# Moving the norm of two attention heads and half of the output projection into the end of the attention loop

## What is computed

```python
proj = rms_norm(x) @ w_in          # lru_x, lru_gate, q, k, v: 512 columns each
y_lru = rglru_group(lru_x, lru_gate, ...)     # short convolution, gates, a scan over time, gelu
w = softmax(q1 @ k1.T) - lam * softmax(q2 @ k2.T)   # causal, 4 heads, 2 x 64 of q and k each
o = w @ v                          # 128 values per head
y_att = rms_norm(o) * head_gain * 0.8
x = x + rms_norm(concat(y_lru, y_att) @ w_out)
x = x + rms_norm(relu(rms_norm(x) @ w_up)**2 @ w_down)
```

## Time and profile before

| | |
|---|---|
| median of 3 runs | 1195.84 us (1195.27 to 1197.99) |
| the profiled execution | 1198.78 us |
| its span, first to last instruction | 1197.0 us |
| PE busy | 1161.9 us, 97% |
| DVE, ACT busy | 641.8 us (54%), 395.6 us (33%) |
| mean granted PE clock | 0.989 of full speed |

### The profile page before, as it was taken

How to read it: one execution, slowest core, us unless ns; L and a number is a source line. 1 busy time by engine, 2 the same in 40 slices (tenths; PEclk the granted TensorE clock), 3 DMA queues, 4 the chain that set the end, 5 groups by cost and what they waited for, 6 DMA issues and landing times.

```text
span 1197.0 us, 13587 instructions
## 1 busy us (share of the span) xinstructions
PE 1161.9 (97%) x5236; PEld 938.4 (78%) x5236; DVE 641.8 (54%) x848; ACT 395.6 (33%) x666; POOL 34.6 (3%) x47
## 2 busy tenths in 40 slices
PE   7999899999978999999999999999999999999997
PEld 6888787777655788878888888888888888888886
DVE  6666745755743646744444444444444544544458
ACT  7434723545554236641121121122122112112122
POOL 0300000000010100200000000000000000000000
PEclk9999999999988999999999999999999999999999
DMA  6111223112100354021111121121011111111112
GB/s 231 43 36 62 103 90 91 42 36 53 53 1 1 128 168 144 1 88 53 36 55 51 35 70 37 34 70 53 33 55 53 53 35 53 53 35 53 53 53 105
DMA packets 21094, 74.74 MB, mean 62 GB/s; under 512 B 2832, under 2 KB 2960, under 8 KB 20928
## 3 DMA queue, kind: packets, MB, share of 16 engines
q1 hardware_dynamic: 17568, 63.45, 15.9%
q0 software_dynamic: 1664, 6.49, 1.6%
q10 hardware_dynamic: 1824, 4.29, 1.6%
HBM read 65.82 MB, written 4.19 MB: 58 GB/s over the span
## 4 chain that ended last, share of the span: by engine, by line
PE 91%; DVE 4%; ACT 2%; issue 1%; DMA 1%; SPq 0%; ACTq 0%; DVEq 0%
PE pair L307 27%; PE pair L309 27%; PE pair L308 27%; PE pair L616 3%; PE pair L649 3%; PE pair L633 1%; PE pair L619 1%; DMA raw<-weights 1%; DVE negmax L1408 1%; PE pair L465 1%; PE pair L688 1%; ACT wh L863 0%; PE pair L658 0%; ACT dec L944 0%; DVE probs L1402 0%
## 5 line engine op out<-in xcount | busy, mean ns | idle before, releaser
L1595 DVE TENSOR_TENSOR yacc<-yacc,pair 128x1024 f32<-128x1024 f32 x112 | 136.7, 1220 | 133.0 <-PE pair L309 133.0
L307 PE MATMUL pair<-yh,wh 128*128 128x512 f32 x512 | 199.6, 390 | 1.9 <-DVE yl L1522 1.2
L309 PE MATMUL pair<-yh,wl 128*128 128x512 f32 x512 | 199.2, 389 | 0.0
L308 PE MATMUL pair<-yl,wh 128*128 128x512 f32 x512 | 199.2, 389 | 0.0
L308 PE MATMUL pair<-wdl,xh 128*128 128x512 f32 x480 | 187.0, 390 | 0.0
L307 PE MATMUL pair<-wdh,xh 128*128 128x512 f32 x480 | 187.0, 390 | 0.0
L309 PE MATMUL pair<-wdh,xl 128*128 128x512 f32 x480 | 186.8, 389 | 0.0
L1583 DVE TENSOR_TENSOR relu<-relu 128x512 f32<-128x512 f32 x64 | 44.3, 692 | 213.4 <-ACT xh L1164 213.4
L863 ACT ACTIVATE wdh<-raw 128x1024 fp32r<-128x1024 f32 x30 | 30.3, 1053 | 278.5 <-PE pair L309 274.4
L1232 DVE TENSOR_TENSOR wl<-raw,wh 128x1024 fp32r<-128x1024 f32 x70 | 85.4, 1221 | 61.4 <-ACT wh L863 61.4
L1161 ACT ACTIVATE relu<-pair 128x512 f32<-128x512 f32 x64 | 38.3, 598 | 228.8 <-PE pair L309 228.8
(11 more groups left out here) (208 smaller groups left out, 1464.5 us busy)
## 6 DMA issues: line engine op xcount, KB each, us to landing
raw<-weights SPq DMA_DIRECT2D x104, 512.0 KB, 3.3
x_sb<-x SPq DMA_DIRECT2D x8, 512.0 KB, 7.7
q_rot<-q_sb ACTq DMA_DIRECT2D x32, 128.0 KB, 2.4
out<-h_sb SPq DMA_DIRECT2D x7, 512.0 KB, 2.6
x_a<-x POOLq DMA_DIRECT2D x4, 512.0 KB, 5.6
x_b<-x POOLq DMA_DIRECT2D x4, 512.0 KB, 6.9
cos_t<-rope POOLq DMA_DIRECT2D x1, 1024.0 KB, 5.1
gw_raw<-gate_weights POOLq DMA_DIRECT2D x1, 512.0 KB, 3.6
```

What stands on the lines that cost most here:

```text
L307: pe.matmul(o, a_hi, b_hi, start=first, stop=False)
L308: pe.matmul(o, a_hi, b_lo, start=False, stop=False)
L309: return pe.matmul(o, a_lo, b_hi, start=False, stop=last)
L1595: dve.tensor_tensor(y, y, pair[2 + t % 2][:, :], ALU.add).then_inc(y_added, 1)
```

## The change

Five things change.

- **Second half of the values.** ACT makes the high part of piece P_VB ahead of the four square roots of the scan instead of behind them, and that of P_VB+1 ahead of the value copies. DVE makes the low parts one place earlier in its scan loop.
- **Norm of heads 0 and 1 inside the last head's steps.** At step 21 DVE adds epsilon for 16 of the 32 columns and ACT takes their roots; at steps 24 and 25 DVE makes the reciprocals and the diagonals; at steps 25 to 28 PE spreads one half of a head per step into bank 4, and DVE multiplies it (`spread_half`, `early_norm`). ACT copies the high parts at steps 28 and 30, DVE subtracts the low parts at steps 29 and 31. The diagonals of these heads lie in memory of their own.
- **Low parts of P_OUT and P_OUT+1.** DVE makes them at steps 26 and 27 instead of 18 and 22.
- **First step of each head.** At s = 8, 16 and 24 DVE now combines the step before ahead of taking the new maxima.
- **Recurrent half of the output projection, quarter 0.** Its 48 matmuls are cut in four parts of 12 (`out_part`): ahead of the last step's transposes, behind its value products, and around the last sum of squares. Only the spreads of heads 2 and 3 stay behind the attention, now between the two chunks of j = 2. ACT loads the square root's table at s = 32 by a small operation.

```diff
-        diag = sb("diag", [P, 2, T], F32, at_s)
+        diag = [sb("diag01", [P, 2, T], F32, at_x + 40 * KB), sb("diag23", [P, 2, T], F32, at_s)]
...
+        head_mix = [28, 30]
+
+
+        EARLY_NORM = 2 * TT
+        spread_at = [25, 26, 27, 28]
...
+                if j >= EARLY_NORM // 2:
+                    pe.wait_ge(head_var, 1)
...
+            def spread_half(h, hf):
+
+                pe.wait_ge(diag_done, h + 1)
+                pe.wait_ge(q_copied, UNITS)
+                if h + hf:
+                    pe.wait_ge(o_norm_half, 2 * h + hf)
+                pe.matmul(bank(4), ones[:, :], diag[0][:, h, HALF * hf:HALF * hf + HALF], start=True,
+                          stop=True).then_inc(spread_done, 1)
+
+            def out_part(j, tiles):
+
+                pe.wait_ge(w_lo, P_OUT + j + 1)
+                pe.wait_ge(lru_mixed, LC)
+                for kk in range(2):
+                    k = 2 * j + kk
+                    w_cols = slice(HALF * kk, HALF * kk + HALF)
+                    for t in tiles:
+                        if k == 0:
+                            pe.wait_ge(exped, 2 * (steps - 1) + t // 2 + 1)
+                        tok = slice(P * t, P * t + P)
+                        mm = mm3(pe, bank(t), xh[:, mixed_slot(k), tok], xl[:, mixed_slot(k), tok], wh[j][:, w_cols],
+                                 wl[j][:, w_cols], k == 0, False)
+                return mm
...
                     score_step(s)
                 project(filler)
+                if s in spread_at:
+                    spread_half(*divmod(spread_at.index(s), 2))
+                if s == steps:
+                    out_part(0, (0, 1))
...
+            out_part(0, (2, 3)).then_inc(piece_used, 1)
             sumsq_step(steps // 2 - 2)
             for part in range(2):
                 pv_step(steps // 2 - 1, part)
+            out_part(1, (0, 1))
             sumsq_step(steps // 2 - 1)
+            out_part(1, (2, 3)).then_inc(piece_used, 1)
...
 
...
-                if h >= 2:
-                    pe.wait_ge(o_norm, h - 1)
+                pe.wait_ge(o_norm_half, 4)
...
-            for quarter in range(3):
+            for j in range(2, 4):
+                pe.wait_ge(w_lo, P_OUT + j + 1)
+                for kk in range(2):
+                    pe.wait_ge(mix_lo, 2 * j - 4 + kk + 1)
+                    if j == 2 and kk == 1:
+                        spread(2)
+                        spread(3)
+                    token_piece(j % 2, j, range(4), 0, None, mixed_slot, (kk,))
+            for quarter in range(1, 3):
                 for j in range(4):
                     pe.wait_ge(w_lo, P_OUT + 4 * quarter + j + 1)
-                    if quarter == 0:
-
-                        if j < 2:
-                            pe.wait_ge(lru_mixed, LC)
-                        else:
-                            pe.wait_ge(mix_lo, 2 * j - 2)
-                        if j == 1:
-                            spread(0)
-                            spread(1)
-                        if j == 2:
-                            spread(2)
-                            spread(3)
...
                     hi_early(P_VA + 2 + c)
+            hi_early(P_VB)
             for c in range(LC):
                 act.wait_ge(bsq_done, c + 1)
                 act.activation(u_t[:, c, :], u_t[:, c, :], ACT.Sqrt).then_inc(sqrt_done, 1)
-            hi_early(P_VB)
...
             act.wait_ge(rstd_ready, 1)
+            hi_early(P_VB + 1)
             v_copies(0)
-            for j in range(1, N_V):
+            for j in range(2, N_V):
...
+            def head_roots(n):
+
+                cs = slice(EARLY_NORM * n, EARLY_NORM * n + EARLY_NORM)
+                act.wait_ge(head_var, n + 1)
+                act.activation(hroot[:, cs], hvar[:, cs], ACT.Sqrt).then_inc(head_root, 1)
...
                 if s < steps:
                     exp_step(s)
+                else:
+                    act.activation(root[:, 0:1], ones[:, 0:1], ACT.Sqrt)
...
+                if s == EARLY_NORM + 5:
+                    head_roots(0)
+                if s in head_mix:
+                    h = head_mix.index(s)
+                    act.wait_ge(o_norm_half, 2 * h + 2)
+                    act.activation(xh[:, h, :], qk(2 * h), ACT.Copy).then_inc(head_hi, 1)
...
+            hi_early(P_OUT + 2)
             o_step(steps // 2 - 1)
-            act.wait_ge(head_var, 1)
-            act.activation(hroot[:, :], hvar[:, :], ACT.Sqrt).then_inc(head_root, 1)
-
-            for h in range(HEADS):
-                if h % 2 == 0:
-                    hi_early(P_OUT + 2 + h // 2)
-                act.wait_ge(o_norm, h + 1)
-                act.activation(xh[:, h, :], qk(2 * h), ACT.Copy).then_inc(mix_hi, 1)
+            head_roots(1)
+            hi_early(P_OUT + 3)
+            for h in range(2, HEADS):
+                act.wait_ge(o_norm, h - 1)
+                act.activation(xh[:, h, :], qk(2 * h), ACT.Copy).then_inc(head_hi, 1)
...
+            lo_early(P_VB)
...
+                lo_early(P_VB + 1 + c)
                 dve.wait_ge(scan_step, 2 * c + 2)
                 dve.wait_ge(gelu_done, LC)
                 dve.tensor_tensor(gel[:, c, :], u_t[:, c, :], gel[:, c, :], ALU.mult).then_inc(lru_done, 1)
-                lo_early(P_VB + c)
-            lo_early(P_QK)
...
+            def head_vars(n):
...
+                dve.wait_ge(sumsq_done, EARLY_NORM // 2 * (n + 1))
+                dve.wait_ge(o_copied, EARLY_NORM // 2 * (n + 1) + 1 - n)
+                dve.scalar_tensor_tensor(hvar[:, cs], head_sums[:, cs], 1.0 / P, sum0_eps[:, cs], ALU.mult,
+                                         ALU.add).then_inc(head_var, 1)
+
...
+            def diagonals(h):
+                for t in range(TT):
+                    ins = dve.tensor_scalar(diag[h // 2][:, h % 2, P * t:P * t + P], ident[:, :],
+                                            hrstd[:, TT * h + t:TT * h + t + 1], None, ALU.mult)
+                ins.then_inc(diag_done, 1)
+
+            def early_norm(s):
+
+                if s == EARLY_NORM + 5:
+                    head_vars(0)
+                if s == EARLY_NORM + 8:
+                    dve.wait_ge(qk_bank, UNITS)
+                    head_rstd(0)
+                    diagonals(0)
+                if s == EARLY_NORM + 9:
+                    diagonals(1)
+                if s in spread_at:
+                    n = spread_at.index(s)
+                    h, hf = divmod(n, 2)
+                    q = qk(2 * h)[:, HALF * hf:HALF * hf + HALF]
+                    dve.wait_ge(spread_done, n + 1)
+                    dve.scalar_tensor_tensor(q, q, head_gain[:, 0:1], bank(4), ALU.mult,
+                                             ALU.mult).then_inc(o_norm_half, 1)
+                if s - 1 in head_mix:
+                    h = head_mix.index(s - 1)
+                    dve.wait_ge(head_hi, h + 1)
+                    dve.tensor_tensor(xl[:, h, :], qk(2 * h), xh[:, h, :].bitcast(F32),
+                                      ALU.subtract).then_inc(mix_lo, 1)
+
...
-                max_first = s < steps and s % TT < TT // 2 and s % 2 == 0
+                max_first = s < steps and 0 < s % TT < TT // 2 and s % 2 == 0
...
+                    if s == (unit_end(2 * n + 1) + 1 if n < 6 else 20 + n):
+                        lo_early(P_QK + n + 2)
                     if s == unit_end(2 * n + 1) + 1:
-                        lo_early(P_QK + n + 2)
                         rope_cos(n)
...
-            link(dve.tensor_tensor(sum0_eps[:, :], sum0[:, :], sum0[:, :], ALU.mult))
-            link(dve.tensor_scalar(sum0_eps[:, :], sum0_eps[:, :], EPS, None, ALU.mult))
-            dve.wait_ge(sumsq_done, steps // 2)
-            dve.scalar_tensor_tensor(hvar[:, :], head_sums, 1.0 / P, sum0_eps[:, :], ALU.mult,
-                                     ALU.add).then_inc(head_var, 1)
-            dve.wait_ge(head_root, 1)
-            rsqrt_post(hvar[:, :], hroot[:, :], ht1[:, :], ht2[:, :], hrstd[:, :])
...
-            def diagonals(h):
-                if h >= 2:
-                    dve.wait_ge(spread_done, 2 * (h - 1))
...
-            for h in range(0, HEADS, 2):
-                diagonals(h)
-                diagonals(h + 1)
-                lo_early(P_OUT + 2 + h // 2)
-                for n in range(h, h + 2):
-                    dve.wait_ge(spread_done, 2 * n + 2)
-                    dve.scalar_tensor_tensor(qk(2 * n), qk(2 * n), head_gain[:, 0:1],
-                                             pair[2 + n % 2][:, :], ALU.mult, ALU.mult).then_inc(o_norm, 1)
-                for n in range(h, h + 2):
-                    dve.wait_ge(o_norm, n + 1)
-                    dve.wait_ge(mix_hi, LC + n + 1)
-                    dve.tensor_tensor(xl[:, n, :], qk(2 * n), xh[:, n, :].bitcast(F32),
-                                      ALU.subtract).then_inc(mix_lo, 1)
+                early_norm(s)
+
+            lo_early(P_OUT + 2)
+            head_vars(1)
+            head_rstd(1)
```

(12 more changed lines are left out.)

23 lines of the change are left out of this document (15 added, 8 removed).

## The result

The changed kernel takes 1185.87 us (median of 4 runs, 1184.89 to 1186.3), the kernel before, on the same chip in the same minutes, 1196.85 us (1195.27 to 1197.99). The ratio is 0.9909, with a 95% interval of 0.9897 to 0.9921: 11.0 us faster. Forecast was 1185.6 us. The profiled execution took 1185.46 us.

A forecast was written before the change was run, and what follows sets the result against it. PE was taken as the bound, 91% of the last-ending chain over 1197.0 us. Terms -4.9 + 4.0 - 5.0 - 1.1 - 3.6 + 0.4 = -10.2 us, off the median 1195.84, gave 1185.6 us; range 1181.0 to 1191.0.

The forecast's parts named there:

- Values, -4.9: Second half of the values: PE's wait for P_VB's low part and the half clock behind it go, -4.9 us.
- The rival that the wait only moves: At the values, P_VB+1 is late instead, so the 4.9 us are not won: 1190.5 us, chance 0.04.
- Roots at step 21, +2.8: Two table loads and a root delay step 22's exp and so PE's scores of step 23: +2.8 us.
- drain: Rival at the table switches: each holds ACT for longer than its load, 2.6 us more, 1188.2 us; chance 0.02.
- Step 24, -1.3: At step 24 the combine of step 23 goes ahead of the maxima and PE gets it earlier: -1.3 us.
- The clock of the loop, +0.6: PE's longer idle at step 22 may cost clock: +0.6 us, between 0 and 1.7.
- Spreads, +1.9, and the low parts at nothing: Steps 25 to 28: PE's spread halves cost +1.9 us; DVE's low parts fit where it waits anyway.
- The loop in all, +4.0: Whole last-head loop: 2.8 - 1.3 + 1.9 + 0.6 = +4.0 us, with ends 0 and +8.
- Behind the last scores, -5.0 and -1.1: Behind the last scores, moved matmuls fill PE's four gaps, -5.0 us, and the half-clock loss goes, -1.1 us.
- Spreads off the path, -3.6, changes of matmul kind, +0.4: Heads 0 and 1 spreads leave PE's path behind the attention, -3.6 us; four more matmul-kind changes cost +0.4.
- The cover that goes: Norm chain of heads 2 and 3 has less matmul cover but just fits, margins 0.3 and 0.2 us.
- Half clock through the last head, 0.05: Rival: PE stays at half clock from 324.14 to 375 us, +18 us, total 1203 us; chance 0.05.

The follow-up runs named there:

- experiment 1: The kernel before with only the new order of the value pieces (P_VB and P_VB+1 made earlier on ACT and DVE): 1189.45 us.
- experiment 3: The changed kernel with the epsilon and roots of heads 0 and 1 at step 20 instead of 21: 1182.94 us.
- experiment 7: The changed kernel with the low parts of P_OUT and P_OUT+1 at steps 18 and 22 again, as before: 1183.75 us.
- experiment 6: The changed kernel with the maxima ahead of the combine again at steps 8, 16 and 24: 1188.12 us.
- experiment 11: The changed kernel with eight useless matmuls added on PE behind each of steps 22 and 23: 1187.80 us; its profiled run 1183.15 us.
- Experiment 4: The changed kernel with GpSimd's four recurrent low-part subtractions cut to 8 of 1024 columns each, output less exact: 1182.02 us.
- Experiment 2: The changed kernel with the four parts of the recurrent half put back behind the last sum of squares: 1192.18 us.
- experiment 5: The kernel before with the new value order and the four recurrent parts moved, but all four heads normed behind the attention: 1194.43 us.
- experiment 8: The changed kernel with roots at step 20, low parts at 18 and 22, and ACT's recurrent copies at 22, 25, 26, 27: 1179.18 us.
- experiments 9: The kernel before with the new value order alone, plus four useless matmuls on PE behind each of steps 22 to 30: 1192.91 us.

## Why the prediction was right, and where not

The total was right to 0.3 us of the measured median, and sign and range held; none of the rivals came as a whole. Term by term:

- *Values, -4.9:* right. 4.98 us in the change's trace; 5.0 in experiment 1's at the values, though only 3.7 of them at step 22; -4.9 at equal clock. The rival that the wait only moves is refuted: PE has no wait there.
- *Roots at step 21, +2.8:* right in kind. The load at 318.94 starts 0.01 us behind ACT's copy and the operation behind each load at most 0.02 us behind it, so no drain shows on either side. Scores 23 came 3.8 us late against step 22: a DMA issue of ACT ahead of the exp took 1.46 us, 0.85 more than in the kernel before and in experiments 3 and 7, which the prediction could not know. That the median of experiment 3 gives 2.9 us back is near the term partly by luck, since its roots at step 20 still cost 0.8 us.
- *Step 24, -1.3:* right. PE's wait went from 2.12 to 0.79 us, and experiment 6 gives 1.5 at equal clock.
- *The clock of the loop, +0.6:* **the step that failed.** I priced the longer wait alone, from the gap at the values. Behind the 4.94 us of idle, scores, transposes and products took 3.7 us more than at full clock (4.77, 1.72 and 2.68 against 2.97, 0.95 and 1.54 in experiment 11). Half of it went into the 2.08 us that PE waited there before; 1.8 us reached scores 24 (10.01 us from scores 23 on, 8.20 in experiment 11). After that the clock was 1.00 for the rest of the head, and this I had at nothing: the kernel before takes 38.2 us from the transposes of step 23 to the last value products, the same instructions of experiment 1 take 33.8, and 1.4 us of those are half clock at their start (3.51 us up to scores 25, for 2.11 in the change). So a clock of 1.00 throughout is worth some 5.8 us there, an estimate. Both are larger than the term, and opposite.
- *Spreads, +1.9, and the low parts at nothing:* **mis-sized.** I asked only whether DVE was free, not who else worked then. Eight diagonals, a weight's low part and a head's low part fell beside GpSimd, and PE had two new waits of 1.1 us for DVE. Experiment 4 prices this at 3.9 us, 3.65 of them in this stretch; experiment 7 prices the moved low parts at 2.1, part of it the same loss. The spreads themselves were cheaper than forecast: without GpSimd the stretch takes 32.96 us with them, and 33.8 less 1.4 without them at full clock, so about 0.5 us, an estimate.
- *The loop in all, +4.0:* 2.7 in the profiled pair, which is 3.8 (exp) + 1.8 (half clock at scores 23) - 1.3 (step 24) - 5.8 (better clock later) + 0.5 (spreads) + 3.7 (GpSimd). So the near hit is luck: two costs and one larger gain that nobody forecast almost cancel. The gain is not the change's own to claim, since experiment 1 has most of it without a single spread.
- *Behind the last scores, -5.0 and -1.1:* right. Experiment 2 undoes it for 6.3 us.
- *Spreads off the path, -3.6, changes of matmul kind, +0.4:* the tail gained 10.8 us in all where -9.3 was the sum. The estimate of 0.1 for a change of kind holds: behind the first matmul of each of the four parts the next starts 0.31 to 0.33 us later, for 0.23 within a part. The slow clock of before was worth 1.5 us, not 1.1 (20.4 us from the last value products of the loop to the first spread, for 18.9 in experiment 1). The rest, some 0.7 us, is not split up.
- *The cover that goes:* right, with more room than I had worked out: 0.75 us ahead of the spreads. That the cover matters is what experiment 5 shows from the other side.
- *Half clock through the last head, 0.05:* did not come. Its place was right; a window at 0.62 is there, but the clock was back at 1.00 from 335 us on.

The total itself needs the same caution. The medians differ by 11.0 us, the kernels at equal clock by 9.6, the profiled pair by 13.3: a forecast of 10.2 is right by each of them to about 3 us, and to 0.3 us only by the first.

Of the signs named ahead, the one on scores 23 came out otherwise: 3.8 us later against step 22, not 2.8; and quarter 0 ended 13 us earlier in the profiled pair, not 10.

## What to carry to other kernels

Before moving work into an engine's idle time, look at who else is active in that window, not only at whether the engine is free: here four short GpSimd instructions took 3.9 us from a change worth 11. Work that fills one gap can have been the cover of another, as in experiment 5; look what it covered before moving it. And when kernels differ by a few us with PE partly idle, compare them at the same granted clock, or the clock's part, 4.4 us of the last head in experiment 1, is read into the edit.

## What the runs showed of the hardware

- **GpSimd holds up VectorE's work from SBUF to SBUF.** Beside a GpSimd subtraction of 2.35 us from SBUF, DVE's work from SBUF to SBUF grew by 1.8 to 2.1 us (diagonals 1.66 to 3.75, low part 1.22 to 3.03). A reduction from PSUM beside it in the kernel before did not (1.29 and 1.28), nor did a product with one input from PSUM (0.74 us at 346.24 in experiment 8, with GpSimd busy from 345.84 to 348.20). The Trainium skill says this (SBUF — State Buffer, "SBUF: two separate sides"): the port pair that GpSimd shares with VectorE's operations in a two-port mode or with two SBUF inputs is a lock, not a share of bandwidth, and whoever comes second is blocked. The trace agrees, by nearly the whole length of GpSimd's operation, though it doesn't show the mode of the diagonals, which have one large input; I had not read the page against this change.
- **The same code at another clock.** 46 executions of one kernel spread over 7 us, and their span follows the mean granted clock at 0.69 us for each 0.001. The same instructions of the last head took 49.4, 47.1 and 45.0 us in the kernel before and experiments 5 and 1, by where the clock fell to 1.2 GHz. Behind the same idle 1.16 us at 191 us, with the same matmuls to follow, it fell to 0.50 in the profiles of experiments 3 and 5, at a cost of 1.5 us, and stayed at 1.00 in the others. Less idle time doesn't make it predictable (experiments 9 and 11).
- **A DMA issue of ACT is not always 0.6 us.** In the loop up to step 22, single issues took 1.12 to 1.96 us in seven of the thirteen profiles (1.46 in the change at 315.01, none over 0.7 in the kernel before), and the work behind them on ACT came as much later. Nothing here shows why.
- **A table load costs its 1.28 us and no more,** also twice in a row: the load at 318.94 us ends at 320.22, the root starts at 320.24, the next load at 320.47, the exp at 321.76.
